# A second layer's mixing stages that carry the first layer's context experts, two selections to eight 64x64 matmuls

## The chip, the cores and the metric

The kernel runs on one core of one Trainium2 chip. The metric is the device time of one execution in microseconds (us); the kernel before takes 5878.68 us, the median of three runs.

## The reference, cut to what matters

Two layers of one trunk work on 512 latent tokens and 256 context tokens of width 1024. A layer mixes its tokens by attention, a short convolution and a long (FFT) convolution, merges the three, and then sends every token through experts:

```
x = x + gt1 * _merge(gates, y_att, y_sc, y_hy, ...)
h2 = _rmsnorm(x, g_norm2) * (1 + sc2) + sh2
# _peer: per token and each of 8 heads, the 16 best of 128 x 128 experts
a = gelu(einsum('chkd,cd->chk', u_tab[e], hc))
f = einsum('chk,chkd->cd', g * a, v_tab[e])       # e: 8 heads x 16 experts
x = x + gt2 * f
```

Layer 0 does this for latents and context. Layer 1 needs the context only as keys and values of its attention, and its experts run for the latents alone. So nothing of layer 1 before the attention's keys and values reads what layer 0's context experts give. Layer 1's modulation, filter spectra, latent norm, convolution branches and long convolutions read the latents or weights alone.

## The kernel before, in words

The kernel is a row of stages. Each is a `Phase`: a block in which every engine has an instruction queue of its own, in written order, joined by semaphores, with a barrier of all engines at its end. For layer 1 the stages and their starts are: `phase_mod` (3464.1), `phase_norm1` (3555.4), `phase_qkv` (3583.5), `phase_attention` (3638.2), `phase_conv_branches` (3729.9), then `phase_spectrum` and `phase_long_conv` for two orders (3873.9, 3932.1, 3973.2, 4031.1), `phase_merge` (4071.2), `phase_out`, `phase_norm2`, `phase_query`, `phase_experts` (4451.0) and `phase_final` (5865.2). Layer 0 has the same stages for latents and context; its experts run from 1365.3 to 3464.1.

**Experts.** A tile is 128 tokens, one to a partition. A unit is one tile and one head; it has 16 selections. A selection is one expert for each of the 128 tokens: POOL gathers 128 rows of 8 KB (the expert's u and v) into one of 8 slots (line 1739), DVE multiplies the u half with the token's vector and sums it (`dot`, 1843), ACT takes the GELU of that column (1773), DVE scales the identity with gate and activation (`weigh`, 1851), and PE adds diagonal times v half into PSUM, as two 128x512 float32 matmuls (1755). Between the dots DVE finds the next unit's experts in five pieces (`topk_parts`, 1791 to 1836). A slot is free when its two matmuls are done (`slot_used`). Layer 0 has 6 tiles, thus 768 selections; layer 1 has 4, thus 512.

**Weights.** They are split into a rounded high and a low part. `SplitRing` loads a block by SP (288), ACT rounds it (296), POOL subtracts (262). In `phase_conv_branches` SP loads block n + slots once job n is projected; ACT waits in its queue for that block to land before it goes on (`round_ahead`); PE does 24 matmuls for a job (953). In `phase_mod` 24 chunks of 1 MB are loaded (439), rounded by ACT (455), split by DVE (262) and multiplied (495).

**Attention** already uses parts of PE's array: scores take 64 rows by 128 columns (836), the two heads of a pair in the two row halves, and values take 128 rows by 64 columns (860).

Of the kernel before, what the change touches and what calls it, by code (L numbers as in the profile page):

```python
# [27 lines left out]
P = 128  # L28
# [8 lines left out]
HEADS, KV_HEADS, HD = 8, 2, 64  # L37
PAIRS = HEADS // 2
# [100 lines left out]
class Phase:  # L139
# [4 lines left out]
    def __init__(self, nc):  # L144
        self.nc, self.sems = nc, []
        Phase.count += 1
        self.tag = f"p{Phase.count}"
# [6 lines left out]
    def __enter__(self):  # L154
        self.stack = ExitStack()
        self.block = self.stack.enter_context(self.nc.Block())
        return self
# [8 lines left out]
class Chip:  # L166


    def __init__(self, nc, ctx, io):
        self.nc, self.io = nc, io  # L170
        self.arena_at, self.views = (nc.sbuf_base + 31) // 32 * 32, {}
        self.arena = ctx.enter_context(nc.sbuf_tensor("arena", [P, 201 * 256], F32))
# [160 lines left out]
def filter_hidden(c):  # L333

    return c.at(107, T_ALL)


class FilterMlp:


    def __init__(self, c, ph, layer, width):
        self.c, self.layer, self.width = c, layer, width
        self.z, self.h1, self.h2 = c.at(160, T_ALL), c.at(163, T_ALL), filter_hidden(c)
        self.a, self.r = c.at(166, 2, T_ALL), c.at(172, T_ALL)
        self.w1, self.w2 = c.at(176, FH), c.at(176.25, FH)
# [3 lines left out]
    def sync(self, sp):  # L349
        io, layer = self.c.io, self.layer  # L350
        sp.dma_start(self.z[0:EMB, :], io["feat"]).then_inc(self.landed, 16)
# [3 lines left out]
    def tensor(self, pe, i):  # L355
# [6 lines left out]
        for lo, hi in ((0, L_LAT), (L_LAT, self.width)):  # L362
            if lo < hi:
                last = self.c.nc.tensor.matmul(self.c.psum[0:FH, (2 + 2 * i) * 512 + lo:(2 + 2 * i) * 512 + hi], w,
                                               x[:, lo:hi], start=True, stop=True)
        last.then_inc(self.summed, 1)

    def vector(self, dve, i):
# [3 lines left out]
        at = (2 + 2 * i) * 512  # L372
        c.nc.vector.tensor_scalar(self.a[0:FH, i, 0:self.width], c.psum[0:FH, at:at + self.width], c.cols[0:FH, b:b + 1],
                                  c.cols[0:FH, b + 1:b + 2], ALU.add, ALU.mult).then_inc(self.shifted, 1)

    def gpsimd(self, pool):

        nc, st = self.c.nc, Steps(pool, self.steps)
        r, w = self.r[0:FH, 0:self.width], slice(0, self.width)
        for i in range(2):  # L380
            a, part = self.a[0:FH, i, w], self.z[0:FH, w]
            pool.wait_ge(self.shifted, i + 1)
            if i:
                pool.wait_ge(self.sined, 1)
            st.do(nc.gpsimd.tensor_scalar(r, a, 1.0 / TWO_PI, ROUND, ALU.mult, ALU.add))
            st.wait()
            st.do(nc.gpsimd.tensor_scalar(r, r, ROUND, None, ALU.subtract))
            st.wait()
            for piece in (PI_HI, PI_MID, PI_LO):
                st.do(nc.gpsimd.tensor_scalar(part, r, piece, None, ALU.mult))  # L390
                st.wait()
                st.do(nc.gpsimd.tensor_tensor(a, a, part, ALU.subtract))
                st.wait()
            nc.gpsimd.tensor_scalar(r, a, PI_F32, -PI_F32, ALU.min, ALU.max).then_inc(self.reduced, 1)

    def scalar(self, act, i):
        act.wait_ge(self.reduced, i + 1)
        self.c.nc.scalar.activation((self.h1, self.h2)[i][0:FH, 0:self.width], self.r[0:FH, 0:self.width],
                                    ACT.Sin).then_inc(self.sined, 1)


def phase_mod(c, layer, full):
# [18 lines left out]
    with Phase(nc) as ph:  # L421
# [4 lines left out]
        mlp = FilterMlp(c, ph, layer, T_ALL if full else L_LAT)  # L426
# [17 lines left out]
        def _(act):  # L444
# [6 lines left out]
            for n in range(2 * chunks):  # L451
# [17 lines left out]
                if n in (12, 23):  # L469
                    mlp.scalar(act, n // 23)  # L470
# [3 lines left out]
        def _(pool):  # L474
            mlp.gpsimd(pool)
# [31 lines left out]
        def _(dve):  # L507
# [21 lines left out]
            for t in range(NT):  # L529
# [3 lines left out]
                c.mod[:], c.psum[:, 7 * 512:7 * 512 + 2 * N_MOD].rearrange("p (j s) -> p j s", s=2),  # L533
                c.cols[:, C_BMOD:C_BMOD + N_MOD].unsqueeze(2).to_broadcast([P, N_MOD, 2]), ALU.add))
# [96 lines left out]
def phase_qkv(c, layer, full):  # L631

    nc, io = c.nc, c.io
    qT, kT, vN = c.at(116, PAIRS, T_ALL), c.at(128, KV_HEADS, T_ALL), c.at(134, NT, P)
    sqb = c.at(143, 2, 640)
    qn = c.at(148, 2, 640)
    qr = c.at(153, 2, 640)
# [1368 lines left out]
```

## Time and profile before

| what | value |
|---|---|
| median of three runs | 5878.68 us (5877.49 to 5885.24) |
| the profiled execution's own time | 5882.08 us |
| its span | 5880.3 us |
| busy: PE, DVE, POOL, ACT | 78%, 63%, 33%, 21% |
| moved by DMA | 1503.39 MB, 256 GB/s in the mean |
| of that by gathers (queue q0) | 1342.26 MB |

The profile cuts the span into 40 slices and gives the busy share of each engine and of the 16 DMA engines in each. A table by stage says more than the mean over the span here, since stages have different limits. A duration of a matmul record is longer than the distance to the next, because matmuls are pipelined; and a float32 matmul leaves two records.

### The profile page before, as it was taken

What the parts mean: (1) busy time and instruction counts of PE and PEld (TensorE: products, weight loads), DVE (VectorE), ACT (ScalarE), POOL (GpSimd) and SP (SyncE); (2) the same over time, 40 slices, a digit from 0 to 9 for tenths busy, and PEclk for the clock granted to TensorE, in tenths of its full rate; (3) what the DMA queues carried; (4) which work ended last, traced back from release to release, by engine and by line L of the source; (5) the groups of instructions that cost most, each with busy time, mean ns of one, the idle gap of its engine ahead of it and who ended that gap; (6) DMA issues with size and microseconds to landing.
All of it is one profiled execution on the core that took longest, in us unless ns stands there. A gap on an engine that the chain in (4) does not pass through costs nothing. (4 is left out here: it accounts for less than half of the span.)

```text
span 5880.3 us, 55023 instructions
## 1 busy us (share of the span) xinstructions
PE 4560.4 (78%) x14456; PEld 2499.2 (43%) x14456; DVE 3701.1 (63%) x8357; ACT 1235.2 (21%) x2648; POOL 1947.4 (33%) x1532
## 2 busy tenths in 40 slices
PE   6899879887776777777777777988977777777776
PEld 3585358764222332323322325745853222322322
DVE  6613442235777877877877776344135777877877
ACT  5521022212111111111111134412222111111111
POOL 4021013212343443444444432211423334444443
PEclk8999889988889888888888888999978889888888
DMA  5011012116999999999999981111316999999998
GB/s 219 15 58 47 15 37 64 61 36 256 381 385 399 383 381 388 394 385 380 397 385 383 397 356 46 58 47 36 97 53 272 379 380 398 377 381 396 383 378 344
DMA packets 223040, 1503.39 MB, mean 256 GB/s; under 512 B 25284, under 2 KB 25668, under 8 KB 51852
## 3 DMA queue, kind: packets, MB, share of 16 engines
q0 software_dynamic: 184320, 1342.26, 56.4%
q1 hardware_dynamic: 38412, 157.98, 7.4%
q8 instruction: 77, 1.26, 0.1%
q14 instruction: 231, 1.89, 0.1%
HBM read 1498.04 MB, written 2.10 MB: 255 GB/s over the span
## 5 line engine op out<-in xcount | busy, mean ns | idle before, releaser
L1755 PE MATMUL psum<-arena 128*128 128x512 f32 x5120 | 2552.2, 656 | 957.0 <-DVE arena L1851 951.3
L1739 POOL DMA_INDIRECT arena<-in_uv,arena x1280 | 1419.9, 1109 | 2059.1 <-PE psum L1755 1718.4
L1755 PEld LDWEIGHTS psum<-arena 128*128 128x128 f32 x5120 | 1041.2, 210 | 2467.2 <-DVE arena L1851 1359.2
L1843 DVE SCALAR_TENSOR_TENSOR arena<-arena 128x1024 f32<-128x1024 f32 x1280 | 1554.1, 1219 | 249.5 <-issue 194.0
L953 PE MATMUL psum<-view_at,view_at 128*128 128x512 f32 (+1 forms) x4896 | 951.1, 357 | 18.5 <-issue 9.7
L953 PEld LDWEIGHTS psum<-view_at,view_at 128*128 128x128 f32 x4896 | 814.3, 190 | 152.0 <-issue 20.7
L1773 ACT ACTIVATE arena<-arena 128x1 f32<-128x1 f32 x1280 | 252.3, 202 | 2927.2 <-DVE arena L1843 2926.3
L262 POOL TENSOR_TENSOR view_at<-view_at,view_at 128x1024 fp32r<-128x1024 f32 (+1 forms) x184 | 397.1, 2168 | 1369.8 <-ACT view_at L296 1368.5
L1851 DVE TENSOR_SCALAR arena<-ident,arena 128x128 f32<-128x128 f32 x1280 | 450.8, 352 | 57.0 <-ACT arena L1773 48.8
L1488 DVE TENSOR_TENSOR view_at<-view_at,psum 128x768 f32<-128x768 f32 (+1 forms) x48 | 39.4, 820 | 372.9 <-PE psum L953 372.9
L1877 DVE TENSOR_TENSOR arena<-psum,arena 128x1024 f32<-128x1024 f32 x80 | 98.0, 1224 | 267.7 <-PE psum L1755 267.7
L262 DVE TENSOR_TENSOR view_at<-view_at,view_at 128x2048 fp32r<-128x2048 f32 (+5 forms) x122 | 198.5, 1652 | 75.8 <-ACT view_at L455 48.8
L296 ACT ACTIVATE view_at<-view_at 128x1024 fp32r<-128x1024 f32 (+1 forms) x172 | 159.7, 938 | 387.0 <-DMA view_at<-in_w_in 253.9
L1773 ACT ACT_TABLE_LOAD x120 | 154.0, 1283 | 11.3 <-issue 9.9
L495 PE MATMUL psum<-view_at,cond 128*4 128x512 f32 x384 | 110.8, 431 | 47.3 <-ACT view_at L455 27.8
L1538 PE MATMUL psum<-view_at,view_at 128*128 128x512 f32 x480 | 116.3, 406 | 33.1 <-POOL view_at L262 33.1
L1197 PE MATMUL psum<-arena 128*128 128x512 f32 x288 | 126.2, 594 | 4.2 <-DVE arena L1235 4.2
L1802 DVE COPY arena<-arena 128x256 f32 (+1 forms) x82 | 23.3, 284 | 158.0 <-POOL arena L1727 158.0
L670 PE MATMUL psum<-view_at,view_at 128*128 128x256 f32 (+1 forms) x528 | 98.0, 349 | 29.6 <-PEq L163 29.6
L1538 PEld LDWEIGHTS psum<-view_at,view_at 128*128 128x128 f32 x480 | 94.3, 197 | 54.6 <-issue 29.5
L1796 DVE MAX8 arena<-arena 128x8 f32<-128x128 f32 (+1 forms) x246 | 83.3, 339 | 37.5 <-DVE arena L1794 36.5
L1764 ACT ACT_TABLE_LOAD x82 | 105.2, 1283 | 2.8 <-PEq L163 1.4
(185 smaller groups left out, 3549.2 us busy)
## 6 DMA issues: line engine op xcount, KB each, us to landing
view_at<-in_w_in SPq DMA_DIRECT2D x108, 512.0 KB, 3.5
view_at<-in_w_mod SPq DMA_DIRECT2D x48, 1024.0 KB, 11.6
arena<-in_uv,arena POOLq DMA_INDIRECT x1280, 9.2
view_at<-in_w_br SPq DMA_DIRECT2D x48, 256.0 KB, 2.6
arena<-in_dft SPq DMA_DIRECT2D x2, 4096.0 KB, 15.1
view_at<-in_w_out SPq DMA_DIRECT2D x16, 512.0 KB, 7.4
view_at<-in_wq SPq DMA_DIRECT2D x16, 512.0 KB, 3.5
arena<-in_x SPq DMA_DIRECT2D x1, 2048.0 KB
```

What stands on the lines that cost most here:

```text
L262: return eng.tensor_tensor(lo, x, hi.bitcast(F32), ALU.subtract)
L296: self._high(act, lambda out, x: self.c.nc.scalar.activation(out, x, ACT.Copy), n)
L495: last = nc.tensor.matmul(c.bank(q % 2, 512, 4), c.cond4[:, half * HALF + k], part[:, n % 2, k * 512:(k + 1) * 512], start=(half == 0 and ...
L953: last = nc.tensor.matmul(c.psum[:, bank * 512 + lo:bank * 512 + hi], a[:, k], b[:, k, lo:hi], start=(k == 0 and i == 0), stop=(k == kt - ...
L1197: last = nc.tensor.matmul(out, table, hw[:, t, src * W_BR:(src + 1) * W_BR], start=(i == 0), stop=(i == nt - 1))
L1538: last = nc.tensor.matmul(c.bank(2 * (t % 4) + h), a[:, k, t * P:(t + 1) * P], b[:, 4 * h:4 * h + 4, k, :], start=(k == 0 and i == 0), sto ...
L1739: nc.gpsimd.indirect_dma_start(out=slots[k % RING], out_offset=None, in_=table, in_offset=bass.IndirectOffsetOnAxis(ap=eidx[:, p, k:k + 1] ...
L1755: last = nc.tensor.matmul(c.bank(2 * p + h), diag[:, k % 4], slots[k % RING][:, D + h * 512:D + (h + 1) * 512], start=(k == 0), stop=(k == ...
L1764: nc.scalar.activation(exps[:, p], topc, ACT.Exp, bias=small[:, p, 0:1], accum_out=small[:, p, 1:2]).then_inc(exp_done, 1)
L1773: nc.scalar.activation(gelus[:, p, k:k + 1], dots[:, p, k:k + 1], ACT.Gelu).then_inc(gelued, 1)
L1843: nc.vector.scalar_tensor_tensor(out=junk[:, k % 2], in0=slots[k % RING][:, 0:D], scalar=1.0, in1=h2N[:, bass.ds(t, 1)].rearrange("p a n - ...
L1851: nc.vector.tensor_scalar(diag[:, k % 4], c.ident[:], gelus[:, p, k:k + 1], probs[:, p, k:k + 1], ALU.mult, ALU.mult).then_inc(diag_ready, 1)
```

## The change

- **Layer 0's experts** stage does the 4 latent tiles only. The 256 selections of the 2 context tiles go to a class `CtxExperts`.
- **`context_beside`** runs layer 1's modulation, both spectra, the latents' norm, the convolution branches and both long convolutions with a `Share` of those selections in each: 48, 40, 40, 12, 88, 12 and 16. After each step of a stage, every engine goes on in its own queue with gathers (up to 3 ahead of the dots), dots, weights (1 behind) or sums (2 behind, in pairs).
- **Slots** are 6 instead of 8. One buffer takes the dot's product.
- **Halves exchanged.** For every second selection the indices and probabilities are written with partitions 0 to 63 and 64 to 127 exchanged (by DVE, in more instructions), and the dot is taken with a copy of the tile whose halves are exchanged. Each diagonal is then two 64x64 diagonals side by side, and a pair of selections is summed by eight 64x64x512 matmuls on the four quarters of the array, into banks 4 to 7. `add_tile` adds both pairs of banks to x.
- **ACT** scales the activation and makes the diagonal (three instructions for a selection, each waiting on the one before); DVE did it before.
- **Modulation beside**: 3 slots instead of 7, the splits by DVE and POOL in turn.
- **Spills.** SBUF runs short: the two spectra, the latents' x and the short convolution's result are stored to DRAM and loaded again; the DFT tables are loaded in halves. The order is now spectra, norm, convolutions, long convolutions, then the context's norm in a stage of its own, then qkv and attention. The ring of convolution weights has 3 slots instead of 4.
- **Merge** of layer 1 uses the split h as it stands, and does not restore and split it again.

```diff
@@ class CtxExperts, new
+    RING, SUM_LAG, FETCH = 6, 2, 3
+    def gather(self, pool, n):
+        for i in range(self.n_gathered, self.up_to(n, self.FETCH)):
...
+            if i >= self.RING:
+                pool.wait_ge(self.slot_used, i - self.RING + 1)
+                pool.sem_inc(self.turn, 1)
+            nc.gpsimd.indirect_dma_start(
...
+    def weigh(self, act, n):
+        for i in range(self.n_weighed, self.up_to(n, -1)):
...
+            act.wait_ge(self.dotted, i + 1)
+            nc.scalar.activation(self.gelus[:, q, k:k + 1], self.dots[:, q, k:k + 1], ACT.Gelu).then_inc(self.act_steps, 1)
...
+            nc.scalar.activation(self.scaled[:, q, k:k + 1], self.gelus[:, q, k:k + 1], ACT.Copy,
+                                 scale=self.probs[:, q, k:k + 1]).then_inc(self.act_steps, 1)
...
+            nc.scalar.activation(self.diag[:, i % 4], self.ident2, ACT.Copy,
+                                 scale=self.scaled[:, q, k:k + 1]).then_inc(self.diag_ready, 1)
...
+    def sum_up(self, pe, n):
+        for i in range(self.n_summed, self.up_to(n, -self.SUM_LAG) // 2 * 2, 2):
...
+            pe.wait_ge(self.diag_ready, i + 2)
+            for h in range(2):
+                for rows, others, bank in ((TOP, BOTTOM, 4 + h), (BOTTOM, TOP, 6 + h)):
+                    for k, tokens in ((i, rows), (i + 1, others)):
+                        last = nc.tensor.matmul(self.c.psum[tokens, bank * 512:(bank + 1) * 512], self.diag[rows, k % 4],
+                                                self.slots[k % self.RING][rows, D + h * 512:D + (h + 1) * 512],
...
+            last.then_inc(self.slot_used, 2)
...
+class Share:
+    def place(self, s, part=0, parts=1):
+        return self.first + self.n * (s * parts + part + 1) // (self.steps * parts)
...
@@ phase_conv_branches, each engine's loop over the jobs
+            for n in range(len(jobs)):
+                share.gpsimd(pool, n)
+                if n + lay.ring_slots < len(jobs):
+                    ring.split(pool, blocks=(n + lay.ring_slots,))
...
+                feature_job(c, ring.parts(n), STRIDE * (n % SLOTS), width, KD, (lay.hT_high, lay.hT_low),
+                            after=lambda k: share.tensor(pe, n, k, KD)).then_inc(proj, 1)
...
@@ context_beside, new
+    phase_mod_beside(c, nxt, lay, Share(experts, 0, 48, 24))
+    for order in range(2):
+        phase_spectrum(c, nxt, L_LAT, order, lay, Share(experts, 48 + 40 * order, 88 + 40 * order, 13), spectra[order])
...
+    phase_conv_branches(c, nxt, lay, Share(experts, 140, 228, 24), [(keep_ysc, lay.ysc)])
...
+    for order, (first, last) in enumerate(((228, 240), (240, 256))):
+        kept = spectra[order]
+        phase_long_conv(c, L_LAT, order, lay, Share(experts, first, last, 7 + 2 * order),
...
@@ phase_experts
-    nt = NT if full else NT_LAT
+    nt = NT_LAT
```

## Rows read from the trace of the kernel before

**Rows 1.** The page's 40 slices: DMA share in tenths, and GB/s.

```profile
DMA  5011012116999999999999981111316999999998
GB/s 219 15 58 47 15 37 64 61 36 256 381 385 399 383 381 388 394 385 380 397 385 383 397 356 46 58 47 36 97 53 272 379 380 398 377 381 396 383 378 344
```

**Rows 2.** The windows view, by stage; the columns are named in its first line.

```profile
core 0: us, PE busy (x) PEld busy (x) DVE busy (x) ACT busy (x) POOL busy (x), PEclk, DMA share, GB/s
1365.30:3464.10 2098.80, 1528.08 (x3072) 625.31 (x3072) 1659.55 (x4262) 325.95 (x987) 852.02 (x769) 0.87 0.95 384
3464.10:3555.40 91.30, 70.85 (x292) 27.73 (x292) 64.71 (x41) 62.31 (x54) 46.07 (x18) 0.85 0.69 278
3555.40:3583.50 28.10, 9.29 (x48) 7.97 (x48) 25.75 (x34) 13.72 (x22) 10.28 (x4) 0.62 0.29 112
3729.90:3873.90 144.00, 134.76 (x608) 111.32 (x608) 36.66 (x45) 42.29 (x56) 53.98 (x23) 0.98 0.22 73
3873.90:3932.10 58.20, 55.16 (x118) 22.84 (x118) 20.74 (x24) 7.41 (x9) 0.00 (x0) 0.87 0.22 82
3932.10:3973.20 41.10, 30.80 (x72) 13.55 (x72) 22.15 (x34) 1.20 (x2) 0.00 (x0) 0.96 0.00 0
3973.20:4031.10 57.90, 54.33 (x118) 22.00 (x118) 20.74 (x24) 7.41 (x9) 0.00 (x0) 0.88 0.03 9
4031.10:4071.20 40.10, 30.71 (x104) 20.11 (x104) 22.86 (x42) 1.53 (x4) 0.00 (x0) 0.96 0.00 1
4451.00:5865.20 1414.20, 1024.11 (x2048) 415.87 (x2048) 1112.72 (x2854) 218.33 (x659) 568.21 (x513) 0.87 0.94 380
```

**Rows 3.** Layer 1's experts, line 1739 (gathers): its instructions and their time to landing.

```profile
L1739 POOL DMA_INDIRECT arena<-in_uv,arena x488: 932/938/2004, 4469.4 to 5797.4; - x163
...
DMA to landing us min/median/max: 5.2/9.3/16.6
```

**Rows 4.** Groups of instructions by line and shape, layer 1's experts.

```profile
L1843 DVE SCALAR_TENSOR_TENSOR arena<-arena 128x1024 f32<-128x1024 f32 x512 | 621.7, 1219 | 109.4 <-issue 82.3 <-DMA arena<-in_uv,arena 25.2
L1773 ACT ACTIVATE arena<-arena 128x1 f32<-128x1 f32 x512 | 101.2, 202 | 1176.7 <-DVE arena L1843 1176.3
L1773 ACT ACT_TABLE_LOAD x48 | 61.6, 1283 | 4.4 <-issue 3.9
L1843 DVE DVE_READ_ACCUMULATOR arena<-arena 128x1 f32 x512 | 41.7, 82 | 0.0
```

**Rows 5.** Timeline, start of layer 1's experts: one unit's topk, first gather and dots.

```profile
4451.52 0.29 DVE L1802 COPY arena<-arena 128x256 f32<-128x256 f32 x1 [64.39 <-POOL arena L1727]
...
4462.19 0.23 DVE L1836 TENSOR_SCALAR arena<-arena 128x16 f32<-128x16 f32 x1
4463.10 1.06 POOL L1739 DMA_INDIRECT arena<-in_uv,arena  x1 [11.63 <-issue]
...
4468.71 1.23 DVE L1843 SCALAR_TENSOR_TENSOR arena<-arena 128x1024 f32<-128x1024 f32 x1 [6.29 <-DMA arena<-in_uv,arena]
```

**Rows 6.** Timeline of PE: layer 0's experts, then layer 1's attention.

```profile
1502.45 12.28 PE L1755 MATMUL psum<-arena 128*128 128x512 f32 x28 [1.84 <-DVE arena L1851]
...
3692.98 1.56 PE L836 MATMUL psum<-arena 64*128 64x512 f32 x8
3694.47 1.53 PE L849 MATMUL psum<-ident,arena 128*128 128x128 f32 x12
...
3700.44 2.81 PE L860 MATMUL psum<-arena 128*64 128x256 f32 x24
```

**Rows 7.** Groups by line and shape, layer 1's convolution branches.

```profile
L262 POOL TENSOR_TENSOR view_at<-view_at,view_at 128x1024 fp32r<-128x1024 f32 x20 | 47.9, 2396 | 143.4 <-ACT view_at L296 143.4
L296 ACT ACTIVATE view_at<-view_at 128x1024 fp32r<-128x1024 f32 x20 | 21.2, 1061 | 59.7 <-DMA view_at<-in_w_in 59.7
```

**Rows 8.** The same view, layer 1's modulation.

```profile
L262 DVE TENSOR_TENSOR view_at<-view_at,view_at 128x2048 fp32r<-128x2048 f32 x24 | 58.2, 2432 | 24.1 <-ACT view_at L455 24.0
```

**Rows 9.** The same view, layer 1's norm.

```profile
L600 ACT ACTIVATE view_at<-view_at 128x256 fp32r<-128x256 f32 x8 | 3.3, 413 | 3.8 <-DVE view_at L613 3.8
```

More of the change, by code:

```diff
@@ new lines, with __init__, tensor, vector @@
+class Share:
+    def __init__(self, experts=None, first=0, last=0, steps=1):
+        self.experts, self.first, self.n, self.steps = experts, first, last - first, steps
+    def place(self, s, part=0, parts=1):
+        return self.first + self.n * (s * parts + part + 1) // (self.steps * parts)
+    def tensor(self, pe, s, part=0, parts=1):
+        if self.experts:
+            self.experts.sum_up(pe, self.place(s, part, parts))
+    def vector(self, dve, s):
+        if self.experts:
+            self.experts.dot(dve, self.place(s))
+    def scalar(self, act, s):
+        if self.experts:
+            self.experts.weigh(act, self.place(s))
+    def gpsimd(self, pool, s):
+        if self.experts:
+            self.experts.gather(pool, self.place(s))
@@ L975, in phase_conv_branches @@
     SLOTS = 3
-    TB = 3072
-    with Phase(nc) as ph:
-        ring = SplitRing(c, ph, conv_blocks(c, layer), ahead=4)
+    STRIDE = 512 * -(-width // 512)
+    TB = SLOTS * STRIDE
+    with Phase(nc, gathers=share.experts is not None) as ph:
+        ring = SplitRing(c, ph, conv_blocks(c, layer), at=lay.ring_at, slots=lay.ring_slots, ahead=lay.ahead)
         restored, proj, a_done, cx_ready, sc_done, conv_done, turned, kept, steps = (ph.sem(s) for s in (
             "restored", "projected", "act_done", "cx_ready", "sc_done", "conv_done", "transposed", "turned_kept", "dve_steps"))
-        mirrored = ph.sem("mirrored")
+        mirrored, stored = ph.sem("mirrored"), ph.sem("stored")
         def cols(base, tap, tile, tiles):
@@ L1006, in _ @@
         def _(pool):
-            ring.split(pool)
-            pool.wait_ge(proj, len(jobs))
-            restore(nc.gpsimd, range(5, KD))
+            ring.split(pool, blocks=range(lay.ahead, lay.ring_slots))
+            for n in range(len(jobs)):
+                share.gpsimd(pool, n)
+                if n + lay.ring_slots < len(jobs):
+                    ring.split(pool, blocks=(n + lay.ring_slots,))
+            if not lay.apart:
+                pool.wait_ge(proj, len(jobs))
+                restore(nc.gpsimd, range(5, KD))
         @ph.block.tensor
@@ L1121, in dft_views, with phase_spectrum @@
         at += tiles * w / 256
-    out["all"] = c.at(48, int((at - 48) * 256))
+    out["all"] = c.at(first, int((at - first) * 256))
     return out
-def spectrum_views(c, nt):
-    return c.at(152, nt, W_BR), c.at(160, nt, W_BR), c.at(168, W_BR)
 def spectrum_jobs(nt):
     return [(w, f) for f in range(nt) for w in ("re", "im")] + [("top", 0)]
-def phase_spectrum(c, layer, length, order):
+def phase_spectrum(c, layer, length, order, lay, share, keep=None):
     nc, io = c.nc, c.io
@@ L1160, in _ @@
             if order == 0:
-                sp.dma_start(tab["all"], io[f"dft{length}"]).then_inc(tab_in, 16)
+                sp.dma_start(*lay.filter_tables(io, length)).then_inc(tab_in, 16)
+            if keep is not None:
+                for n, (what, ft) in enumerate(jobs):
+                    sp.wait_ge(kept, n + 1)
+                    src, to = {"re": (kre[:, ft], ft), "im": (kim[:, ft], nt + ft), "top": (kre_b, 2 * nt)}[what]
+                    sp.dma_start(keep[:, to], src).then_inc(stored, 16)
+                sp.wait_ge(stored, 16 * len(jobs))
         @ph.block.tensor
@@ L1212, in _ @@
                 nc.scalar.activation(ab[t % 2], hw[:, t], ACT.Abs).then_inc(ab_d, 1)
+            for n in range(len(jobs)):
+                share.scalar(act, nt + n)
+        @ph.block.gpsimd
+        def _(pool):
+            for n in range(nt + len(jobs)):
+                share.gpsimd(pool, n)
         @ph.block.vector
```

801 lines of the change are left out of this document (651 added, 150 removed).

## The prediction, as it was put on record

> **What bounds the kernel now.** I read the 40 slices first. They show two kinds of time [rows 1]: long runs of slices with the DMA engines nine tenths busy and about 385 GB/s, and between them slices that move 36 to 97 GB/s. The windows by stage say which is which [rows 2]. Layer 0's experts take 2098.8 us at a DMA share of 0.95 and 384 GB/s, layer 1's 1414.2 us at 0.94 and 380 GB/s. In both, DVE is busy 79% of the time and PE's records cover 73%; neither is full. A gather of 1.05 MB lands 9.3 us after its issue in the median and 5.2 us at the least [rows 3]: transfers stand in a queue behind each other. So the experts are bound by bytes: 2098.8/768 = 2.73 us a selection, 1.05 MB at 384 GB/s. The mixing stages are the opposite: the convolution branches have PE busy 134.8 of 144.0 us at a DMA share of 0.22, the spectra 55 of 58 us at 0.22 and 0.03, the long convolutions 31 of 41 us with nothing moved. The reader is to see that layer 1's seven stages of this list hold 460.7 us (91.3 + 28.1 + 144.0 + 58.2 + 41.1 + 57.9 + 40.1) in which the DMA engines are mostly idle.
>
> **What is removed.** Layer 0's experts keep 4 tiles, as layer 1's have. Their time is then layer 1's, 1414.2 us, and 2098.8 − 1414.2 = 684.6 us go. The seven stages as they stood, 460.7 us, go as well, and what replaces them must be priced.
>
> **The floor of what replaces them, by bytes.** I take the experts' 385 GB/s. Beside 1.05 MB for each selection the stages move: modulation 24 chunks of 1.05 MB; each spectrum 0.5 MB of inputs and 2.4 MB stored, the first also 2.1 MB of tables; the norm three weight blocks of 0.52 MB and 2.1 MB of x stored; the convolution branches 21 blocks and 1.0 MB stored; the long convolutions 2.4 MB each, the first also 2.1 MB of tables. That is
>
> - modulation, 48 selections: 75.5 MB, 196 us
> - spectra, 40 each: 46.9 and 44.8 MB, 122 and 116 us
> - norm, 12: 16.3 MB, 42 us
> - convolution branches, 88: 104.3 MB, 271 us
> - long convolutions, 12 and 16: 17.1 and 19.2 MB, 44 and 50 us
>
> Together 841 us, against 460.7 + 684.6 = 1145.3 us removed.
>
> **The engines against that floor.** DVE: a dot is 1.22 + 0.08 us [rows 4], with its wait on the dot before about 1.35, times 256 = 346. A unit's topk took 10.9 us from first to last instruction, its waits included [rows 5]; four short instructions more and one copy less make 12, times 16 = 192 (bounds 11 and 13). Two `add_tile` are 8 instructions of a dot's size, 10 us; the exchanged copies of the tile 4 of under 1.2, 4 us. The stages' own DVE work [rows 2], 214, less the 12 splits of 2.43 that go to POOL [rows 8], is 185. Sum 737 us: 88% of the floor, close enough to matter. ACT: the GELU is 0.20 [rows 4]; the two added instructions are not in the trace, a column scaled is 0.20 like it, a 128x64 diagonal lies between 0.20 and the 0.41 of 128x256 [rows 9], and I take 0.25, nearest the small one; with three waits 0.9 us a selection, plus two table loads of 1.28 a unit [rows 4]: 271 us and the stages' own 135. It is not the bound by load. POOL: 0.94 to 1.1 us a gather [rows 2, 3], 270 us; the splits of 24 convolution blocks at 2.4 [rows 7]; 12 of 128x2048, not seen on POOL, twice 2.4 = 4.8 (bounds DVE's 2.43 and 5.2): 58; the filter's 46. Not the bound.
>
> **The eight 64x64 matmuls.** No row shows four quarters of the array at once. The nearest rows are halves [rows 6]: the scores of one unit are 8 records, for two matmuls of 512 and two of 256 columns, in 1.56 us. In the experts' queue 28 records of 512 columns take 12.28 us, 0.43 each, 0.86 for a matmul. Done singly these four would take 0.86 + 0.86 + 0.43 + 0.43 = 2.6 us; in pairs 1.3 plus the drain of the last record, about 0.27, which is what was measured. The values, 128 rows by 64 columns, are 24 records of 256 columns in 2.81 us where singly they take 5.2. So both splits run two at a time, by rows and by columns. I take it that they compose: a pair of selections is then 4 × 0.43 = 1.7 us, about 1.9 with its start, 0.95 a selection where 128x128 needs 1.7. PE in sum: 243 + 386 of the stages' own = 629 us. Bounds: 1.7 us a pair (all four) and 6.9 us (none, 8 × 0.86). TensorE: Matmul & The Clock Gate (the Trainium skill, Measured speedup vs the span model) gives 10.6 times for 16 small tiles, rows and columns composed; by it the pair costs what I take. Against the change speaks the Trainium skill's TensorEngine Tiling (Array Packing), Key Properties: a change of tiling mode drains the engine, and here the mode changes twice a pair. The row shows the start of the 128x128 transposes at 3694.47, before the scores' last record is over at 3694.54; the trace shows no drain longer than that, and the sum by the rule without a price is the same.
>
> **Where the floor is missed.** The experts stage runs free loops over 8 slots. Here every engine meets its share at fixed places of its queue. First the slots: gather i needs the pair of i − 6. From the end of that dot: ACT 0.9, PE 1.9, issue to dot 5.6 with an idle queue [rows 5], one more transfer 2.7, the dot 1.35: 12.5 us for six selections, where bytes take 16.4. Slack is 3.9 us per six, and into this loop fall DVE's topk pieces (2 us each), its own work, and PE's feature matmuls. Second, in the convolution branches, the weight block: ACT waits in its queue for block n + 3, issued when job n is projected. ACT stood idle 59.7/20 = 3.0 us for each [rows 7]; with gathers between I take 5 to 6 (bounds 3.0 and 9.3, the loaded gather). What is queued behind it on ACT is the weighing of job n + 1's selections, which PE needs for its sums, which stand between its feature matmuls: 5.5 + 1.06 (round) + 1.4 (keeps) + 2 (two selections weighed) + 2.6 (pair and last group) = 12.6 us a job, against 11.3 by bytes; 24 jobs = 302, and 13 for fill and end. POOL's split stands in the same chain ahead of gathers. Third, each of the seven barriers empties the pipe for some microseconds, with three gathers in flight to cover them.
>
> By stage I take: modulation 225 (196, and 12 + 6 for the first topk and the first gather [rows 5], 11 for stalls); spectra 130 and 125 (8 us a step each over the serial folding between); norm 50; convolution branches 315; long convolutions 70 and 78, because their chain of PE and DVE (41.1 and 40.1 us alone) is serial, waits for 4.5 and 2.4 MB first and has the dots (25 and 31 us with topk) put into it. Then the context's norm, a stage of its own: half the norm's columns, but 3.1 MB of weights and 3.1 MB restored, 25 us. The sum is 1018 us.
>
> Attention loses POOL's splits beside it, a few us; I take 4. The merge's start is set by its weights as before: nothing. The unchanged stages stay.
>
> 1018 − 460.7 − 684.6 − 4 = −131 us. From the span 5880.3 that is 5749; the profiled execution's own time, 5882.1, lies 3.4 us above the median of the runs and 1.8 above its span, so for the median I say 5748.
>
> **The rivals.**
>
> *Bytes alone.* The queues run ahead of each other well enough and the floor holds but for start and serial ends: 841 + 18 + 25 + 20 = 904, so 5880 − 245 = 5635. For it: before, the experts stage itself reached 0.95 of the DMA share with DVE at 79%. Against it: the fixed places. 0.18.
>
> *Queues that hold each other.* If a weight block takes the loaded gather's 9.3 us, the convolution branches take 16.4 us a job, 394; a like loss of 15% in modulation and spectra adds 70: the middle is 1167, the time about 5898. This decides from a middle of 1149 us on: that is 131 over my sum, 0.5 us for each of the 256 selections. At half that loss it is 5810. I give 0.12 to 5790 to 5868 and 0.08 to the slower part. DMA: Bandwidth & Descriptors (the Trainium skill, Queues, rings and completion order) says that an engine serves its queues in turn; by it a weight block shares with a gather instead of standing behind three, which is my 5 to 6 us. No row here has both queues full.
>
> *The quarters don't run together.* If eight 64x64 matmuls run singly, a pair is 6.9 us, PE's sum is 883 + 386, and with 45 for start and context norm the middle is 1314: 6045. It ends on the other side from 5.6 us a pair on, (1149 − 45 − 386)/128. Against it stand both halves [rows 6]. 0.08. Between them stands a rival from rows: a float32 matmul's two records are of one quarter, so if matmuls start strictly in order the second holds back the next matmul, each starts 0.43 after the last, and a pair is 9 × 0.43 = 3.9 us; PE's sum is 499 + 386 = 885, over the floor, and the time about 5810. But then the scores' eight records would need 1.98 us, and they took 1.56. 0.04. The Trainium skill's TensorE: Matmul & The Clock Gate, Part 3: Packing small matmuls — row/col tiling, has matmuls start strictly in order; by that rule this rival would hold, and the row speaks against it.
>
> **How the numbers follow.** The forecast, 5690 to 5790, has 0.50; bytes alone 0.18; queues 0.12 + 0.08; strict order 0.04; single quarters 0.08. About 0.2% (12 us) is what a measurement can tell from no change. Faster 0.82, same 0.02, slower 0.16. The range reaches from bytes alone, 5632, to the better part of the queues' case, 5865; cases of both signs are in the sum, and the likeliest one's own range is 5690 to 5790.
>
> **What would show it.** In the profile after, layer 0's experts should take about 1414 us, and the DMA share of the 1018 us that follow should be near 0.8, not 0.95 (bytes alone) nor 0.7 (queues). The eight 64x64 matmuls should be 16 records within about 2 us; 4 or 7 us would mean one of PE's rivals. ACT's wait for the convolution's weights should be 5 to 6 us a block. If it is over 9, or POOL's wait for PE fills the stages, the prediction is too low. A dot much over 1.22 us beside POOL's splits would also make it wrong.

## The result, and the profile after

The changed kernel takes 5935.22 us (median of 4 runs, 5930.88 to 5939.88), the kernel before 5878.43 in the same comparison: a ratio of 1.009, 95% interval 1.0075 to 1.0105. It is slower by 0.9%, where 5748 us was forecast, and lies outside the range of 5632 to 5865. The profiled execution took 5930.88 us, its span is 5929.1.

First the page's 40 slices of the changed kernel, to lay beside [rows 1]:

```profile
PEclk8999889988888888888678778879988888888888
DMA  5011012116999999998878866750315999999998
GB/s 217 15 58 46 14 39 61 61 36 270 371 371 393 372 373 391 372 373 352 322 288 321 313 241 266 285 189 17 96 59 224 385 387 397 387 380 398 381 384 343
```

The eight slices in which layer 1's stages carry gathers move 189 to 322 GB/s, not the 385 of the experts, and PE's granted clock is 0.6 to 0.8 there. The windows by stage answer to [rows 2]; in order: layer 0's experts, modulation, two spectra, norm, convolution branches, two long convolutions, the context's norm, layer 1's experts.

```profile
core 0: us, PE busy (x) PEld busy (x) DVE busy (x) ACT busy (x) POOL busy (x), PEclk, DMA share, GB/s
1371.30:2808.40 1437.10, 1042.19 (x2048) 424.61 (x2048) 1112.23 (x2854) 217.94 (x659) 562.95 (x513) 0.85 0.92 374
2808.40:3060.80 252.40, 153.57 (x660) 51.88 (x660) 181.81 (x282) 104.22 (x198) 141.99 (x81) 0.68 0.80 309
3060.80:3208.40 147.60, 102.50 (x438) 32.92 (x438) 93.40 (x212) 48.32 (x139) 44.92 (x40) 0.84 0.82 326
3208.40:3352.80 144.40, 103.55 (x438) 33.77 (x438) 91.50 (x201) 51.58 (x143) 45.63 (x40) 0.84 0.80 311
3352.80:3411.00 58.20, 26.13 (x128) 9.71 (x128) 44.67 (x89) 23.96 (x58) 20.72 (x15) 0.65 0.71 262
3411.00:3808.40 397.40, 273.18 (x1312) 144.52 (x1312) 208.77 (x433) 128.30 (x345) 155.44 (x109) 0.82 0.69 265
3808.40:3885.10 76.70, 47.44 (x168) 17.92 (x168) 44.54 (x91) 14.30 (x42) 12.54 (x12) 0.79 0.57 215
3885.10:3961.20 76.10, 52.46 (x248) 25.74 (x248) 47.01 (x78) 15.46 (x55) 13.48 (x13) 0.81 0.60 225
3961.60:3984.50 22.90, 3.67 (x16) 2.91 (x16) 17.65 (x22) 12.46 (x20) 9.81 (x4) 0.57 0.69 275
4508.30:5913.90 1405.60, 1019.86 (x2048) 415.93 (x2048) 1109.49 (x2854) 217.82 (x659) 569.75 (x513) 0.87 0.94 382
```

| part | forecast, us | measured, us | off by |
|---|---|---|---|
| modulation | 225 | 252.4 | +27.4 |
| spectra | 130 + 125 | 147.6 + 144.4 | +37.0 |
| norm | 50 | 58.2 | +8.2 |
| convolution branches | 315 | 397.4 | +82.4 |
| long convolutions | 70 + 78 | 76.7 + 76.1 (and 0.4 between stages) | +5.2 |
| the context's norm | 25 | 22.9 | −2.1 |
| layer 0's experts | 1414.2 | 1437.1 | +22.9 |
| layer 1's experts, as before | 1414.2 | 1405.6 | −8.6 |
| stages ahead of layer 0's experts | as before | | +6.0 |
| attention | −4 | 89.4 where it was 91.7 | +1.7 |

The middle holds 1176.1 us instead of 1018. In sum 180.1 us more than the forecast of −131.3: +48.8 on the span, which is what the spans show (5929.1 − 5880.3). The DMA share of the middle is 0.73, where the prediction said near 0.8, and 0.7 for queues that hold each other. Nearly half of the miss (82.4 of 180.1) lies in one stage, the convolution branches. Its groups by line and shape:

```profile
L643 DVE SCALAR_TENSOR_TENSOR arena<-arena 128x1024 f32<-128x1024 f32 x88 | 129.3, 1469 | 163.2 <-DMA arena<-in_uv,arena 160.4 <-PEq L165 2.4
L529 PE MATMUL psum<-arena 64*64 64x512 f32 x704 | 119.9, 812 | 118.6 <-ACT arena L513 118.5
L264 POOL TENSOR_TENSOR view_at<-view_at,view_at 128x1024 fp32r<-128x1024 f32 x21 | 52.8, 2513 | 159.5 <-ACT view_at L298 159.5
L513 ACT ACTIVATE arena<-arena 128x64 f32<-128x64 f32 x88 | 30.6, 348 | 8.3 <-PE psum L529 5.6
L506 ACT ACTIVATE arena<-arena 128x1 f32<-128x1 f32 x88 | 25.9, 295 | 3.5 <-ACT arena L502 0.4
L298 ACT ACTIVATE view_at<-view_at 128x1024 fp32r<-128x1024 f32 x21 | 22.2, 1057 | 155.8 <-DMA view_at<-in_w_in 155.8
```

ACT waits 155.8 us in 21 blocks, 7.4 us each, for the block of weights (L298). POOL, whose split follows that rounding in the same queue as its gathers, waits the same time (159.5). DVE then waits 160.4 us for gathers, and PE 118.5 us for ACT's diagonals. One wait shows on four engines. Compare [rows 7], where ACT's wait was 3.0 us a block and hidden.

The quarters of the array do run together. PE's timeline in the middle of this stage:

```profile
3602.95 3.69 PE L529 MATMUL psum<-arena 64*64 64x512 f32 x16 [6.04 <-ACT arena L513]
3606.58 3.92 PE L1500 MATMUL psum<-view_at,view_at 128*128 128x512 f32 x12
3610.43 1.95 PE L529 MATMUL psum<-arena 64*64 64x512 f32 x16
```

Sixteen records take 1.95 us at a granted clock of 1.00, the 2.4 GHz level, and 3.69 us at 0.50, the 1.2 GHz level, after PE had stood idle for 6 us.

The groups of the modulation, to lay beside [rows 8]:

```profile
L643 DVE SCALAR_TENSOR_TENSOR arena<-arena 128x1024 f32<-128x1024 f32 x48 | 96.9, 2019 | 43.8 <-DMA arena<-in_uv,arena 43.2
L264 POOL TENSOR_TENSOR view_at<-view_at,view_at 128x2048 fp32r<-128x2048 f32 x12 | 54.3, 4526 | 4.1 <-ACT view_at L935 3.8
L587 DVE SCALAR_TENSOR_TENSOR arena<-arena 128x8 uint32<-128x8 f32 x4 | 15.8, 3943 | 0.1
```

A dot has a mean of 2019 ns where it takes 1219 [rows 4], and an instruction on 8 columns (L587) has a mean of 3.9 us. The slow ones are few: the median dot takes 1226 ns, and those that stand beside a split of POOL (4526 ns) make the mean. The longest of the 48, in the timelines of POOL and DVE:

```profile
2989.53 4.50 POOL L264 TENSOR_TENSOR view_at<-view_at,view_at 128x2048 fp32r<-128x2048 f32 x1
2993.98 1.27 POOL L743 TENSOR_TENSOR arena<-arena 64x512 f32<-64x512 f32 x1
2989.64 6.70 DVE L643 SCALAR_TENSOR_TENSOR arena<-arena 128x1024 f32<-128x1024 f32 x1 [2.99 <-DMA arena<-in_uv,arena]
```

It starts 0.11 us behind POOL's split and ends 1.1 us behind POOL's next instruction.

### The profile page after: what moved, and what is told of

Its sections match the earlier page's. It is cut to its first block and busy times, and to the rows that moved or that the text cites. A ratio compares the mean times of both kernels' runs of the same rounds, so it can differ in the third digit from the quotient of the medians.

```text
span 5929.1 us, 56070 instructions
## 1 busy us (share of the span) xinstructions
PE 4452.6 (75%) x15480; PEld 2394.9 (40%) x15480; DVE 3656.2 (62%) x8105; ACT 1384.3 (23%) x3155; POOL 1979.7 (33%) x1537
## 5 line engine op out<-in xcount | busy, mean ns | idle before, releaser
L2361 PE MATMUL psum<-arena 128*128 128x512 f32 x4096 | 2062.0, 661 | 776.9 <-DVE arena L2457 770.6
L2361 PEld LDWEIGHTS psum<-arena 128*128 128x128 f32 x4096 | 840.5, 211 | 1997.6 <-DVE arena L2457 1090.3
L2449 DVE SCALAR_TENSOR_TENSOR arena<-arena 128x1024 f32<-128x1024 f32 x1024 | 1244.5, 1220 | 193.3 <-issue 144.7
L264 POOL TENSOR_TENSOR view_at<-view_at,view_at 128x1024 fp32r<-128x1024 f32 (+1 forms) x196 | 453.0, 2322 | 1354.5 <-ACT view_at L298 1349.5
L1500 PEld LDWEIGHTS psum<-view_at,view_at 128*128 128x128 f32 x4896 | 819.4, 192 | 203.7 <-issue 72.0
L643 DVE SCALAR_TENSOR_TENSOR arena<-arena 128x1024 f32<-128x1024 f32 x256 | 373.2, 1458 | 315.3 <-DMA arena<-in_uv,arena 282.5
L529 PE MATMUL psum<-arena 64*64 64x512 f32 x2048 | 329.0, 769 | 178.0 <-ACT arena L513 177.8
L2457 DVE TENSOR_SCALAR arena<-ident,arena 128x128 f32<-128x128 f32 x1024 | 362.4, 354 | 51.2 <-ACT arena L2379 42.9
L298 ACT ACTIVATE view_at<-view_at 128x1024 fp32r<-128x1024 f32 (+1 forms) x176 | 163.7, 940 | 485.0 <-DMA view_at<-in_w_in 353.7
L529 PEld LDWEIGHTS psum<-arena 64*64 64x64 f32 x2048 | 80.3, 163 | 351.5 <-ACT arena L513 208.5
L264 DVE TENSOR_TENSOR view_at<-view_at,view_at 128x2048 fp32r<-128x2048 f32 (+5 forms) x102 | 163.9, 1629 | 76.0 <-ACT view_at L2059 35.9
L976 PE MATMUL psum<-view_at,cond 128*4 128x512 f32 x192 | 67.5, 495 | 100.6 <-POOL view_at L264 62.9
L1769 PE MATMUL psum<-arena 128*128 128x512 f32 x288 | 134.6, 611 | 3.5 <-DVE arena L1819 3.5
```

Of the source, the lines that this page charges most:

```text
L264: return eng.tensor_tensor(lo, x, hi.bitcast(F32), ALU.subtract)
L298: self._high(act, lambda out, x: self.c.nc.scalar.activation(out, x, ACT.Copy), n)
L529: last = nc.tensor.matmul(self.c.psum[tokens, bank * 512:(bank + 1) * 512], self.diag[rows, k % 4], self.slots[k % self.RING][rows, D + h ...
L643: nc.vector.scalar_tensor_tensor(out=self.junk, in0=self.slots[i % self.RING][:, 0:D], scalar=1.0, in1=self.h2_turned if i % 2 else self.h ...
L1500: last = nc.tensor.matmul(c.psum[:, at + lo:at + hi], a[:, k], b[:, k, lo:hi], start=(k == 0 and i == 0), stop=(k == kt - 1 and i == 2))
L1769: last = nc.tensor.matmul(out, table, hw[:, t, src * W_BR:(src + 1) * W_BR], start=(i == 0), stop=(i == nt - 1))
```

## The experiments

**One job later.** The theory: the wait for the weight block, which ACT meets in its queue ahead of the selections' weighing, sets the pace of the convolution branches. The edit moves two things by one job: ACT's rounding, and POOL's split, which waits for that rounding ahead of POOL's gathers.

```diff
-                if n + lay.ring_slots < len(jobs):
-                    ring.split(pool, blocks=(n + lay.ring_slots,))
+                late = 1 if lay.apart else 0
+                if n >= late and n - late + lay.ring_slots < len(jobs):
+                    ring.split(pool, blocks=(n - late + lay.ring_slots,))
...
-                    ring.round_ahead(act, n, proj)
+                if not lay.apart:
+                    ring.round_ahead(act, n, proj)
+                elif n:
+                    ring.round_ahead(act, n - 1, proj)
```

> In layer 1's convolution branches alone, ACT rounds weight block n + 2 (not n + 3) after job n, and POOL splits it one job later too, so that the load has one job more to land. Theory (the weight block held in ACT's queue sets the pace): ACT's wait for the blocks, 155.8 us for 21 in the changed kernel, falls under 40, the stage goes from 397 to 340 to 360 us, the whole from 5935 to about 5885 to 5895. Rival (the slots' round of gather, dot, weight and sum sets the pace): the stage loses under 10 us and the waits move to DVE's wait for gathers and PE's wait for diagonals.

Measured: 5829.34 us (5818.51 to 5831.34), a ratio of 0.9899 to the kernel before, interval 0.9883 to 0.9916. The stage in the windows, and then by groups:

```profile
3413.60:3709.90 296.30, 244.57 (x1312) 137.27 (x1312) 215.17 (x433) 130.14 (x345) 159.73 (x109) 0.93 0.91 355
```

```profile
L643 DVE SCALAR_TENSOR_TENSOR arena<-arena 128x1024 f32<-128x1024 f32 x88 | 131.9, 1499 | 65.9 <-DMA arena<-in_uv,arena 62.5 <-PEq L165 2.4
L529 PE MATMUL psum<-arena 64*64 64x512 f32 x704 | 94.5, 656 | 46.0 <-ACT arena L513 45.7
L298 ACT ACTIVATE view_at<-view_at 128x1024 fp32r<-128x1024 f32 x21 | 21.9, 1045 | 0.0
```

The DMA view of the stage gives the median time from issue to landing; in this run and in the changed kernel it has the same line:

```profile
view_at<-in_w_in SPq DMA_DIRECT2D x21, 512.0 KB, 8.8
```

The block lands no sooner, but ACT's wait for it is 0.0. The stage falls from 397.4 to 296.3 us, about twice what was expected. With the wait gone DVE waits 62.5 us for gathers, not 160.4, the DMA share rises from 0.69 to 0.91, and PE, idle less, has a clock of 0.93 and needs 656 ns for a record, not 812. POOL's wait for the rounding falls too, from 159.5 to 35.8 us, so the run doesn't say how much was lost in ACT's queue and how much in POOL's.

**Modulation's splits on DVE.** POOL's 12 splits of 128x2048 go to DVE.

```diff
-                if n % 2:
-                    pool.wait_ge(hi_ready, n + 1)
-                    split(nc, nc.gpsimd, high[n % SLOTS], low[n % SLOTS], raw[n % SLOTS]).then_inc(low_pool, 1)
-                if n % 2 == 0:
-                    dve.wait_ge(hi_ready, n + 1)
-                    split(nc, nc.vector, high[n % SLOTS], low[n % SLOTS], raw[n % SLOTS]).then_inc(low_dve, 1)
+                dve.wait_ge(hi_ready, n + 1)
+                split(nc, nc.vector, high[n % SLOTS], low[n % SLOTS], raw[n % SLOTS]).then_inc(low_dve, 1)
```

> In the modulation stage DVE makes all 24 splits and POOL none. Theory (POOL's tensor instructions hold up DVE's in this stage): the dots' mean there falls from 2.02 us to about 1.3 (the filter's POOL instructions stay), the four index writes from 3.9 us towards 0.2, and although DVE gets 12 x 2.3 = 27 us more, the stage falls from 252 to about 225 to 235 us. Rival (DVE's load sets the pace there): the stage gets longer, 260 to 275 us.

Measured: 5911.36 us (5892.56 to 5920.16), ratio 1.0042, interval 1.0029 to 1.0055; the modulation takes 226.9 us instead of 252.4. The theory's 225 to 235 us is met. Twelve more splits on DVE cost less than POOL's splits did to the stage. A second way to gain is in the same edit: a split takes 2.4 us on DVE and 4.5 on POOL, and PE's wait for splits fell from 64.3 us (62.9 of it for POOL's) to 47.4. How the 25 us divide between the two was not tested.

**Both together.**

> Both edits that helped, together: weight blocks of the convolution branches taken one job later, and the modulation's splits all on DVE. They lie in different stages, so their gains should add: modulation 227 us, convolution branches 296, the whole 5829 - 25 = about 5804 us. Rival (the gathers carried over from one stage to the next couple them): under half of the 25 us shows.

Measured: 5806.25 us (5794.76 to 5815.06), ratio 0.9864, interval 0.9847 to 0.988; modulation 227.5, convolution branches 293.8. The two add up, as expected. Its modulation, by groups:

```profile
L643 DVE SCALAR_TENSOR_TENSOR arena<-arena 128x1024 f32<-128x1024 f32 x48 | 62.7, 1306 | 38.5 <-DMA arena<-in_uv,arena 38.2
L264 DVE TENSOR_TENSOR view_at<-view_at,view_at 128x2048 fp32r<-128x2048 f32 x24 | 55.3, 2305 | 15.2 <-ACT view_at L935 14.7
L587 DVE SCALAR_TENSOR_TENSOR arena<-arena 128x8 uint32<-128x8 f32 x4 | 0.7, 173 | 0.1
```

The dot is back at 1.31 us and the 8-column instruction at 0.17, on the same shapes: it was POOL's splits that held them.

**The stages alone, and the experts alone.** In the first every `Share` is empty and `CtxExperts` is gone, so layer 0's context experts are left out of the computation. In the second all 256 selections run in a stage of their own, then the stages with empty shares.

```diff
-    phase_mod_beside(c, nxt, lay, Share(experts, 0, 48, 24))
+    phase_context_experts(c, Share(experts, 0, 256, 1))
+    phase_mod_beside(c, nxt, lay, Share())
```

> The context's experts are left out; the eight stages run in their new form with no selections beside them. Theory (the stages' new form costs little, the loss is in running both together): they take 480 to 520 us together where 460.7 us stood before, the whole about 5250. Rival (the new form, three slots for weights, splits on POOL, spills and reloads, is itself the cost): over 560 us.

> All 256 context selections run in one stage of their own, with the changed kernel's class, slots and quarters, and the eight stages after it with nothing beside. Theory (bytes bind a free loop with 6 slots as they do with 8): 256 x 2.73 = 700 and 20 for the start, 720 us, so 5250 + 720 = 5970. Rival (six slots and the longer chain dot, three instructions of ACT, pair of sums already fall short of the DMA rate): over 800 us, 6050 or more.

Measured: 5311.28 us without the experts, one run; the new form of the stages takes 122.0 + 63.1 + 64.5 + 26.0 + 140.4 + 54.5 + 49.8 and 21.8 us for the context's norm, 542.1 against the 460.7 of [rows 2]. That is 81 us more, and between what theory (480 to 520) and rival (over 560) expected. Of it 31 are the modulation's and 23 the long convolutions', with their spills and fewer slots. Apart, one run took 6061.96 us: the experts' own stage 765.4 us, 2.99 a selection against 2.73, the stages behind it 541.9. This too lies between theory (720) and rival (over 800): with 6 slots and the longer chain the loop runs at 351 GB/s. In a row the two are 1307 us; the overlap of the changed kernel hides 131 of them, that with rounding one job later 231 (its middle is 1076).

**Four gathers ahead.** `FETCH` is 4 instead of 3.

> The changed kernel with gathers allowed 4 instead of 3 ahead of the dots, 6 slots as before. Theory (in the convolution branches it is the weight block, which stands in ACT's queue and in POOL's ahead of the gathers): more gathers are issued before POOL's split, DVE's wait for gathers there falls from 160 to under 120 us and the stage loses 10 to 30 of its 397 us. Rival (slots are the limit): POOL only waits longer for PE, no stage moves by more than 5 us.

Measured: 5922.98 us, one run. The convolution branches gain 31 us (366.8) and DVE's wait for gathers there falls to 107.4 us, as the theory said; the modulation loses 18 (270.0), the spectra get 4 and 2 us longer (151.8 and 146.3). ACT still waits 138.1 us for weights, POOL now 123.5 for PE. So 31 us come back with ACT's wait nearly as it was, by gathers that POOL issues ahead of its split; the larger part stays.

**Halves not exchanged.** Both selections of a pair take their own quarter; the index and probability instructions and the second copy of the tile go, and `add_tile` reads half of the partitions of each pair of banks.

```diff
-                for rows, others, bank in ((TOP, BOTTOM, 4 + h), (BOTTOM, TOP, 6 + h)):
-                    for k, tokens in ((i, rows), (i + 1, others)):
+                for rows, bank in ((TOP, 4 + h), (BOTTOM, 6 + h)):
+                    for k in (i, i + 1):
...
```

> The halves are not exchanged: a pair of selections is still eight 64x64 matmuls, but all on the two diagonal quarters of the array, and the topk and index writes are the plain ones. If quarters run at once by their place, a pair needs about 3.5 us at full clock instead of 1.95. Theory (PE is not the bound where selections run beside other work): the whole moves by less than 30 us from the 5931 of the changed kernel, lost on PE in the convolution branches and won on DVE's shorter topk. Rival (PE's share is on the path of every slot's round): 60 us or more slower.

Measured: 5954.47 us, one run. PE's timeline in the convolution branches:

```profile
3716.24 3.70 PE L529 MATMUL psum<-arena 64*64 64x512 f32 x16
3727.17 6.33 PE L529 MATMUL psum<-arena 64*64 64x512 f32 x16 [4.29 <-ACT arena L513]
```

The same 16 records take 3.70 us at a granted clock of 1.00 instead of 1.95, 0.46 us for each pair of them, so two quarters at a time; at 0.57 they take 6.33. The middle is 1276.2 us, 100 more than with the exchange: PE's share is on the path, as the rival said. The total is only 19 us up, within the theory's 30, but by luck, since layer 1's experts, whose code is the same, took 1328.3 us instead of 1405.6. Nothing in the theories says why; the last experiments do.

**Stores to DRAM placed alike.** First a rival for layer 0's slower experts: the new buffers in DRAM lie so that the gathers suffer. The kernel before gets the same four buffers and one small store to each.

```diff
+            kept = [nc.dram_tensor("keep_x", (P, NT_LAT, D), F32).ap(), nc.dram_tensor("keep_ysc", (P, KB_BR, L_LAT), F32).ap()]
+            kept += [nc.dram_tensor(f"keep_spectrum{i}", (P, 2 * NT_LAT + 1, W_BR), F32).ap() for i in range(2)]
+            for k in kept:
+                sp.dma_start(k[:, 0, 0:64], y[:, 0, 0:64]).then_inc(stored, 16)
...
```

> The kernel before with the change's four DRAM tensors allocated and a sliver of each stored in the last stage; nothing else. Layer 0's experts took 355 us a tile in the changed kernel and 349 in the kernel before, though the stage's code is the same. If the place of the tables in DRAM is the cause, a tile of layer 0 takes about 355 us here, and the whole is 30 to 40 us over the kernel before. Rival (the arena's 3 KB more, or the stage's length): 349 us and no more than 5 us over.

Measured: 5882.88 us, one run, layer 0's experts 2098.1 us as before. The place in DRAM is refuted as the cause.

**The loop's place.** In [rows 4] the idle time ahead of DVE's dots reads `109.4 <-issue 82.3`. The timeline of the kernel before shows one such wait, right behind the place where the loop over units branches back to its start:

```profile
5601.75 1.23 DVE L1882 TENSOR_TENSOR arena<-arena 128x1024 f32 x1
5607.72 1.23 DVE L1843 SCALAR_TENSOR_TENSOR arena<-arena 128x1024 f32<-128x1024 f32 x1 [4.75 <-issue]
```

The DMA view counts packets on queue q14, of kind instruction: 78 in layer 1's experts before, 79 and 80 in the two experts' stages after, and 5 in the stage that took 1328.3 us. The packets are 8 KB each. In a turn of the loop before, 318 to 320 instructions of DVE, there are five: two within 8.6 us of the branch back, three along the rest of the turn, some 128 instructions apart. So in the next three runs the loops are moved by instructions put ahead of them. 58 increments of a semaphore (on which nothing waits at that count) were put ahead of the loop in layer 0's experts of the kernel before; all code behind them, layer 1's loop too, moves by 58 instructions. The best version (both edits above together) got 44 and 29, the changed kernel 44 and 44.

```diff
             dve.sem_inc(x_added, 1)
+            for _ in range(58 if full else 0):
+                dve.sem_inc(order, 1)
             dve.wait_ge(iota_d, 1)
```

> The kernel before with 58 more semaphore increments on DVE's queue ahead of the loop of layer 0's experts; nothing waits for them. Counted over the trace's DVE records, that loop is 320 instructions long and is at present interrupted by five 8 KB packets of queue q14 in each turn, two of them in the 8.6 us behind the branch back, where DVE stands for 5.5 us, and the packets come 128 instructions apart. In the one stage that showed no such packets in its turns (layer 1's experts of the run without the exchange) the loop crosses two of these 128-instruction steps, in all others three. Theory (the loop's place decides): with the shift both loops cross two steps, q14's packets fall from 119 and 78 to under 20 in each stage, a turn falls from 86.5 and 87.2 us to 81-83.5, and the stages from 2098.8 and 1414.2 us to about 1990 and 1330: 5690 us, a ratio near 0.967. Rival (the stand behind the branch is the loop's own cost, its registers and the branch itself, and the shorter stage came from something else): nothing changes, 5878 us plus under 5 us for the increments.

> The combination run (rounding one job later, the modulation's splits on DVE) with 44 and 29 increments ahead of the two experts' loops. Theory of the loop's place: layer 0's experts fall from 1442.6 to about 1345 us, layer 1's from 1405 to about 1328, the rest stays: 5632 us, a ratio near 0.958 to the kernel before. Rival (the stand is the loop's own): 5806 us. A mixed case (layer 0's loop still crosses three steps, since the place of the steps is read to some 5 instructions only): 5720 us.

> The changed kernel itself with 44 increments ahead of each experts' loop. Theory of the loop's place: 1437 and 1405.6 us become 1345 and 1328, so about 5766 us; against the kernel before with the same cure (5690) the change is then some 75 us slower, 1.3%, where it was 57 us slower as it stands: the loop's place took 23 us from the change in layer 0 but gave more back in the kernel before, whose layer-0 loop makes 24 turns instead of 16. Rival (the stand is the loop's own): 5935 us.

Measured, beside 5880.09 us for the kernel before:

| kernel | us | ratio, 95% interval | layer 0's, layer 1's experts |
|---|---|---|---|
| before, loops moved | 5695.01 | 0.9685 (0.967 to 0.9699) | 1998.9, 1332.2 |
| changed, loops moved | 5762.26 | 0.9799 (0.9784 to 0.9814) | 1332.5, 1339.2 |
| best version, loops moved | 5623.66 | 0.9568 (0.9552 to 0.9583) | 1333.7, 1336.3 |

Windows of both experts' stages of the kernel before with its loops moved, then its dots in layer 1, then the packets of q14 in that stage; [rows 2] and [rows 4] have the first two for the kernel as it was:

```profile
1365.40:3364.30 1998.90, 1510.65 (x3072) 617.75 (x3072) 1657.17 (x4262) 325.59 (x987) 865.05 (x769) 0.90 0.99 403
4336.40:5668.60 1332.20, 1020.71 (x2048) 416.70 (x2048) 1109.14 (x2854) 217.94 (x659) 580.70 (x513) 0.89 0.98 403
```

```profile
L1843 DVE SCALAR_TENSOR_TENSOR arena<-arena 128x1024 f32<-128x1024 f32 x512 | 622.0, 1219 | 27.7 <-DMA arena<-in_uv,arena 25.4
```

```profile
q14 instruction: 3, 0.02, 0.0%
```

The last of these lines in the kernel as it was:

```profile
q14 instruction: 78, 0.64, 0.1%
```

The wait of 82.3 us is gone, 78 packets are 3, and the gathers move 403 GB/s at a DMA share of 0.98 to 0.99. All three kernels came within 9 us of what the theory said, and over 170 us from the rival that the wait is the loop's own; the mixed case of the best version, 5720 us, didn't come. The Trainium skill's Runtime: NRT & Kernel Launch, Instruction fetch mechanics, says that a taken branch to a page outside a window of two forces a fetch before the engine goes on. The trace agrees in kind: two packets come in the 8.6 us behind a branch back, and DVE stands still for some 5 us. The distance between packets, 128 instructions, and their 8 KB are this trace's; the page has blocks of twice that.

## Why the prediction was wrong, point by point

**The step that failed** is "for the weight block 5 to 6", and with it "12.6 us a job" in the convolution branches. ACT's wait was 7.4 us a block, the landing 8.8 us, and 397.4 us are 16.6 for each of 24 jobs. This is the rival "Queues that hold each other", near its number: it gave 16.4 us a job, 394 us, a middle of 1167 (measured 1176.1) and 5898 us. It had 0.08. Part of that nearness is luck. Its 16.4 stands on a wait longer by 3.8 us a block, and the measured one was longer by 1.9 than the 5.5 of the sum; what made up the rest of the 16.6 was not taken apart. And its 70 us for modulation and spectra (measured 64.4) came in modulation mainly from another cause, told below. Moving the wait one job later gives back 101 us of this stage with the same bytes and the same instructions, so the cause is shown: not the bytes and not the load of any engine, but the place of one wait in the queues, in ACT's with the weighing of selections behind it and, through the split, in POOL's with the gathers behind it. Which of the two queues cost more is open: no run moved one without the other. The prediction took the wait as a term to add. With it gone DVE also waited less for gathers and PE's clock was 0.93 instead of 0.82, so the stage came out 19 us under its forecast of 315.

**Modulation**, +27.4: the prediction priced POOL's splits for POOL (4.8 us forecast, 4.53 measured) and not for DVE beside them, though it named a dot much over 1.22 us as a way to be wrong. The dots took 2.02 us in the mean. With the splits on DVE the stage is 227 us, 2 off the forecast. The long convolutions' new form costs 23 us more alone, yet with the experts in it the forecast was met to 5 us.

**Spectra and norm**, +37.0 and +8.2. Alone the spectra take 63.1 and 64.5 us, 12 more in sum than before. In the first spectrum POOL waits 86.8 of 147.6 us for PE to free slots, and a fourth gather ahead changes nothing. That points to the ring of 6 slots and to the place of sums between PE's own matmuls; no experiment took it apart, so its cause is argued and not shown. A part of the ring's length is measured: ACT's two added instructions take 0.295 and 0.348 us, not 0.20 and 0.25.

**Layer 0's experts**, +22.9, and the words "bound by bytes". The prediction gave the stage layer 1's time and called 385 GB/s its floor. With the loops moved both stages of four tiles take 1332 to 1339 us at 401 to 403 GB/s. So the standstill at the loop's branch cost layer 1's experts 82 us before (1414.2 − 1332.2) and layer 0's 105 us in the changed kernel (1437.1 − 1332.5). The row that the prediction quoted [rows 4] had it as the largest idle time. The 22.9 us are gone with it: they were the loop's place and not the change's. A turn with about the same count of packets takes 88.7 us in layer 0 and 86.3 in layer 1 of the changed kernel (medians); why is open.

**What was right.** The eight 64x64 matmuls: 1.95 us forecast as 1.9, 16 records; strict order and single quarters are refuted, and the run without the exchange (3.70 us) shows what the exchange is worth, 100 us of the middle. The Trainium skill's TensorE: Matmul & The Clock Gate, Part 3: Packing small matmuls — row/col tiling, has matmuls start strictly in order, on different tiles about 4 ns apart. Here four records start 6 or 7 ns apart, then four more 0.43 to 0.48 us after them, which agrees with the distance. The rival's reading of that order, that a matmul's second record holds back the next matmul, gave 3.9 us a pair; 1.95 decides against that reading. Which record belongs to which matmul the trace doesn't say, so the order itself is not tested. The context's norm (22.9 for 25), the long convolutions and layer 1's unchanged stages were met too.

**Whether the idea pays** depends on what it is laid beside. Like with like, loops moved in both: the change as made takes 5762.26 us against 5695.01, 1.2% slower; with the rounding one job later and the modulation's splits on DVE it takes 5623.66 us, 1.3% less than the kernel before with its loops moved and 4.3% less than that kernel as it was. In the ratio of 1.009 the loop's place flattered the change a little, since the kernel before makes 24 turns in layer 0's loop and the changed one 16: moving the loops gives 185 us to the first and 173 to the second. The 1.2% and 1.3% are ratios of medians and have no interval of their own.

## What to carry to other kernels

When one engine's queue carries two kinds of work, ask of every wait what of the other kind stands behind it, and put the wait for a transfer as late as its buffer allows: here one job later was worth 1.8% with no instruction removed. Before a share of work is called bound by bytes, read what ends the idle time of its leading engine. Here it was "issue", with packets on an instruction queue at every turn of a loop, and a few dozen instructions of padding removed it. A total hides two effects of opposite sign, so compare stage by stage even where the experiment touches one.

## What the runs showed of the hardware

- DVE's loop of some 319 instructions stands still for some 5 us at each turn (4.75 and 5.5 us read) when its body crosses three of the places at which a packet is drawn on q14, 128 instructions apart. Where it crosses two, q14 shows 3 to 5 packets in the whole stage, not 78 to 119, and the wait is gone. Where the places lie was read from the traces, and the rule forecast three kernels. What sets it inside the engine was not tried.
- In the stage in which POOL ran twelve 128x2048 float32 subtractions (4.5 us each), DVE's dots took 2.02 us in the mean, the longest 6.7, and an 8-column instruction 3.9 us; with the subtractions on DVE they took 1.31 and 0.17. In the convolution branches, with POOL's 128x1024 splits, the dots took 1.47 to 1.50 in the mean.
- Sixteen float32 records of 64x64x512 on four quarters take 1.95 us at 2.4 GHz, 3.69 at 1.2 GHz; on two quarters 3.70 at 2.4 GHz.
- A 512 KB block of weights landed after 3.4 us (median) in the convolution branches before, and after 8.8 us with up to three gathers in flight beside it.
